# Up product with seven short products in pairs 5 to 21, their banks in turn by pair

## The reference

```
    h = _rmsnorm(x, g_pre_ffn[i])
    u = _causal_dwconv(h @ w_up[i], w_conv[i], b_conv[i])
    a, v = u[..., :D_FF], u[..., D_FF:]
    x = x + _rmsnorm((jax.nn.gelu(a) * v) @ w_down[i], g_post_ffn[i])
```

## Time and profile before

| | us |
|---|---|
| median of 3 runs | 1533.89 |
| lowest and highest run | 1531.69, 1535.56 |
| the profiled execution, its own time | 1533.2 |
| its span (first to last instruction) | 1531.3 |
| up product, pairs 4 to 21 (464.69 to 653.98) | 189.29 |

### The profile page before, as it was taken

The page is one execution under the profiler, slowest core; times in us unless marked ns, Lnnn a source line. Parts: engine busy times, 40 slices in busy tenths (PEclk is TensorE's granted clock), DMA queues, the critical chain, the costliest instruction groups (busy, mean ns, idle before and its releaser), DMA issues.

```text
span 1531.3 us, 20288 instructions
## 1 busy us (share of the span) xinstructions
PE 1491.1 (97%) x7953; PEld 1027.9 (67%) x7954; DVE 737.1 (48%) x1252; ACT 532.6 (35%) x975; POOL 556.4 (36%) x373
## 2 busy tenths in 40 slices
PE   8999999999999999999999999999999999999997
PEld 7975677888779999988888777468443443443433
DVE  4156765223785666623335778664533332332334
ACT  5246664223544544421246333424111111111112
POOL 3454555444447666544723362622100010010000
PEclk9999999999999999999999999999999999999999
DMA  8233002222103223352224222368999999999996
GB/s 314 98 110 95 2 2 97 96 97 97 69 33 114 103 83 110 111 188 98 98 84 128 88 81 69 110 250 309 359 429 430 428 427 430 430 429 426 425 425 245
DMA packets 52641, 306.95 MB, mean 200 GB/s; under 512 B 7097, under 2 KB 7353, under 8 KB 40000
## 3 DMA queue, kind: packets, MB, share of 16 engines
q1 hardware_dynamic: 47872, 292.03, 48.8%
q0 software_dynamic: 4096, 11.49, 2.0%
q10 hardware_dynamic: 576, 2.10, 0.3%
HBM read 303.39 MB, written 4.19 MB: 201 GB/s over the span
## 4 chain that ended last, share of the span: by engine, by line
PE 82%; DMA 7%; DVE 7%; ACT 1%; POOL 1%; issue 1%; SPq 0%; DVEq 0%; ACTq 0%
PE banks L535 14%; PE banks L1360 13%; PE banks L580 12%; DMA ring<-experts 7%; PE banks L538 7%; PE banks L1406 5%; PE banks L2693 4%; PE banks L1415 3%; PE banks L2696 2%; PE banks L560 2%; PE banks L2599 2%; PE banks L1160 2%; PE banks L2583 2%; PE banks L2665 1%; PE banks L2569 1%; PE banks L1018 1%
## 5 line engine op out<-in xcount | busy, mean ns | idle before, releaser
L498 POOL TENSOR_TENSOR arena_r<-ring,arena_r 128x1024 fp32r<-128x1024 f32 x125 | 311.9, 2502 | 317.4 <-ACT arena_r L483 297.9
L483 ACT ACTIVATE arena_r<-ring 128x1024 fp32r<-128x1024 f32 x125 | 131.4, 1058 | 320.9 <-PE banks L538 144.3
L1360 PE MATMUL banks<-ring,arena 128*64 128x512 f32 x704 | 223.7, 608 | 12.7 <-DMA ring<-experts 12.7
L535 PE MATMUL banks<-hT_r,arena_r 128*128 128x512 f32 x496 | 194.4, 392 | 0.7 <-ACT arena_r L483 0.4
L535 PE MATMUL banks<-arena_r 128*128 128x512 f32 x496 | 193.3, 390 | 0.0
L580 PE MATMUL banks<-arena_r 128*128 128x512 f32 x784 | 183.5, 389 | 0.6 <-DVE arena_r L525 0.6
L580 PEld LDWEIGHTS banks<-arena_r 128*128 128x128 f32 x784 | 147.1, 188 | 31.6 <-POOL arena_r L498 1.0
L1360 PEld LDWEIGHTS banks<-ring,arena 128*64 128x64 f32 x704 | 70.4, 140 | 144.4 <-issue 143.3
L855 POOL MEMSET arena<- 128x1024 f32 x15 | 14.3, 952 | 340.5 <-PE banks L1313 331.5
L2053 DVE TENSOR_TENSOR resid<-resid,banks 128x1024 f32<-128x1024 f32 x60 | 70.6, 1218 | 129.1 <-PE banks L1415 129.1
L1360 PE MATMUL banks<-arena 128*64 128x512 f32 x278 | 115.9, 595 | 0.0
(11 more groups left out here) (540 smaller groups left out, 2624.1 us busy)
## 6 DMA issues: line engine op xcount, KB each, us to landing
ring<-stream SPq DMA_DIRECT2D x164, 512.0 KB, 3.3
arena<-experts SPq DMA_DIRECT2D x35, 2048.0 KB, 15.9
ring<-experts SPq DMA_DIRECT2D x32, 2048.0 KB, 15.2
ring<-experts SPq DMA_DIRECT2D x17, 1024.0 KB, 18.1
arena<-experts SPq DMA_DIRECT2D x31, 512.0 KB, 11.4
arena<-experts SPq DMA_DIRECT2D x11, 1024.0 KB, 17.3
ring<-experts SPq DMA_DIRECT2D x14, 512.0 KB, 6.8
hT<-experts SPq DMA_DIRECT2D x8, 512.0 KB
```

The costliest lines, as they stand in the source:

```text
L483: nc.scalar.activation(parts(name, m)[:, 0, :], tile(tile_n), ACT.Copy).then_inc(S["w_high"], 1)
L498: nc.gpsimd.tensor_tensor(w[:, 1, :], tile(tile_n), plain(w[:, 0, :]), ALU.subtract).then_inc(S["w_low"], 1)
L535: nc.tensor.matmul(pb[:, bank, :], w[:, 0, k * P:(k + 1) * P], b[:, k, :], start=(k == 0 and part == 0), stop=False)
L1360: last = nc.tensor.matmul(pb[r, bank, :], XT[:, k, r], weights(b, c + e, k * 512, (k + 1) * 512), start=(k == 0), stop=(k == ND - 1))
```

## The change

Mixed are now all pairs from j = 4 to j = 20; plain are 0 to 3 and 21. Pairs 5, 7, ... 19, eight of them, go from plain to mixed. Every pair j, plain or mixed, uses banks 0 to 3 if j is even and 4 to 7 if it is odd. Behind a mixed pair the terms are rounded in their natural order 0 to 6. The token sums t1 to t4 are split one pair later on DVE. The down product starts with token tiles 0, 1 instead of 2, 3.

```diff
-MIXED = range(FIRST_MIXED, NF, 2)
+MIXED = range(FIRST_MIXED, NF - 1)
...
-TERM_ORDER = [4, 5, 6, 0, 1, 2, 3]
+BEHIND_PLAIN, BEHIND_MIXED = [4, 5, 6, 0, 1, 2, 3], list(range(7))
 NQ = len(TERMS)
+
+
+def term_order(j):
+
+    return BEHIND_MIXED if j - 1 in MIXED else BEHIND_PLAIN
...
+        def up_bank(j, w):
+
+            return pb[:, 4 * (j % 2) + w, :]
+
         def term_bank(j, q):
 
             bank, half = PLACES_OF[q]
-            return pb[:, 4 + bank, 256 * half:256 * half + 256]
-
-        def up_bank(j, w):
-
-            if j in MIXED:
-                return pb[:, 4 + w, :]
-            return pb[:, 2 * (PLAIN.index(j) % 2) + w, :]
...
+                if j >= 2:
+                    pe.wait_ge(S["up_dve"], 2 * (j - 2) + 2)
                 if j in PLAIN:
-                    if j >= 2:
-                        pe.wait_ge(S["up_dve"], 2 * PLAIN[PLAIN.index(j) - 2] + 2)
                     for w in range(2):
-                        split_features(pe, "up", 2 * j + w, 2 * (PLAIN.index(j) % 2) + w, hT_r, up_low, 2)
+                        split_features(pe, "up", 2 * j + w, 4 * (j % 2) + w, hT_r, up_low, 2)
                     continue
-                if j > FIRST_MIXED:
-                    pe.wait_ge(S["up_dve"], 2 * (j - 2) + 2)
                 for q in range(NQ - 1):
                     if TERMS[q].split()[1] in ("t1", "t2", "t3"):
                         pe.wait_ge(S["up_sums"], summed(TERMS[q].split()[1], "low"))
                     up_term(j, q).then_inc(S["up_part"], 1)
                 pe.wait_ge(S["up_sums"], summed("t4", "low"))
                 up_term(j, NQ - 1).then_inc(used, 2)
-            split_tokens(pe, "down", S["post_mm"], ((2, 3), (0, 1)), lambda q: pe.wait_ge(S["up_g"], NF - 1 + q))
+            split_tokens(pe, "down", S["post_mm"], ((0, 1), (2, 3)), lambda q: pe.wait_ge(S["up_g"], NF - 1 + q))
...
             def term_high(j, q):
-                if q < 4:
+                if q < 4 and j - 1 in PLAIN:
                     act.wait_ge(S["w_used"], W_UP + 2 * (j - 1) + (1 if q < 2 else 2))
                 elif j == FIRST_MIXED:
                     act.wait_ge(S["w_used"], W_UP)
-                elif q < NQ - 1:
-                    act.wait_ge(S["up_part"], terms_done(j - 2, q))
                 else:
-                    act.wait_ge(S["w_used"], W_UP + 2 * (j - 2) + 2)
+                    before = max(other for other in MIXED if other < j)
+                    act.wait_ge(*((S["up_part"], terms_done(before, q)) if q < NQ - 1 else (S["w_used"], W_UP + 2 * before + 2)))
...
+            for j in range(NF):
+                if j in MIXED:
+                    for q in (6, ) if j - 1 in MIXED else (2, 3):
+                        term_high(j, q)
+                elif j - 1 in PLAIN:
+                    high_act(act, "up", 2 * j + 1)
+                for w in (0, 1) if j - 1 in MIXED else (1, ) if j else ():
+                    conv_last(j - 1, w)
+                if j == 1:
                     x_high("t1")
                     x_high("t2")
-                high_act(act, "up", 2 * j + 3)
-                conv_last(j, 1)
-                gelu(j)
-                if j == 1:
-                    act.wait_ge(S["w_low"], made(W_UP + 3))
+                if j in PLAIN and j + 1 in MIXED:
+                    for q in (4, 5, 6):
+                        term_high(j + 1, q)
+                if j:
+                    gelu(j - 1)
+                if j == 2:
                     x_high("t3")
                     x_high("t4")
-            for q in TERM_ORDER[:5]:
-                term_high(FIRST_MIXED, q)
-            conv_last(FIRST_MIXED - 1, 0)
-            for j in MIXED:
-                for q in TERM_ORDER[5:]:
-                    term_high(j, q)
-                conv_last(j - 1, 1)
-                gelu(j - 1)
-                take_first(j)
-                for w in range(2):
-                    high_act(act, "up", 2 * j + 2 + w)
-                if j + 2 in MIXED:
-                    for q in TERM_ORDER[:3]:
-                        term_high(j + 2, q)
-                for w in range(2):
-                    conv_last(j, w)
-                gelu(j)
-                if j + 2 in MIXED:
-                    for q in TERM_ORDER[3:5]:
-                        term_high(j + 2, q)
+                if j in MIXED:
+                    take_first(j)
+                if j == NF - 1:
+                    high_act(act, "down", 0)
+                elif j + 1 in MIXED:
+                    for q in (0, 1) if j in PLAIN else range(6):
+                        term_high(j + 1, q)
                 else:
-                    high_act(act, "down", 0)
-                conv_last(j + 1, 0)
+                    for w in range(1 if j in PLAIN else 2):
+                        high_act(act, "up", 2 * j + 2 + w)
+                if j in PLAIN:
+                    conv_last(j, 0)
...
                 if j > FIRST_MIXED:
-                    dve.wait_ge(S["w_low"], term_made(j - 2, TERM_ORDER[-1]))
+                    before = max(other for other in MIXED if other < j)
+                    dve.wait_ge(S["w_low"], max(term_made(before, q) for q in (2, 3, 5)))
...
+            for j in range(NF):
+                if j == 2:
                     x_low("t1")
                     x_low("t2")
-                conv(j, 1)
-                gated_rows(j)
-                if j == 1:
+                if j == 3:
                     x_low("t3")
                     x_low("t4")
-            weight_sums(FIRST_MIXED)
-            conv(FIRST_MIXED - 1, 0)
-            for j in MIXED:
-                conv(j - 1, 1)
-                gated_rows(j - 1)
-                for what in ("c11", "u2", "u4", "u3", "c12", "c22", "c21"):
-                    join(j, what)
-                if j + 2 in MIXED:
-                    weight_sums(j + 2)
-                for w in range(2):
-                    conv(j, w)
-                gated_rows(j)
-                if j + 2 not in MIXED:
+                if j - 1 in MIXED:
+                    join(j - 1, "c21")
+                if j in PLAIN and j + 1 in MIXED:
+                    weight_sums(j + 1)
+                for w in (0, 1) if j - 1 in MIXED else (1, ) if j else ():
+                    conv(j - 1, w)
+                if j:
+                    gated_rows(j - 1)
+                if j in MIXED:
+                    join(j, "c11")
+                    if j + 1 in MIXED:
+                        weight_sums(j + 1)
+                    for what in ("u2", "u4", "u3", "c12", "c22"):
+                        join(j, what)
+                if j == NF - 1:
                     dve.wait_ge(S["up_g"], 2)
-                    dve.wait_ge(S["w_low"], term_made(j, TERM_ORDER[-1]))
+                    dve.wait_ge(S["w_low"], split_at(W_UP + 2 * max(MIXED)))
                     split_dve(dve, chain, "down", gT, 0, 2)
-                conv(j + 1, 0)
+                if j in PLAIN:
+                    conv(j, 0)
```

More of the change, by code:

```diff
@@ L146 @@
 TERMS = ["gate_1 x_1", "gate_2 x_2", "s2 t2", "s1 t1", "s3 t3", "s4 x_4", "value_2 t4"]
-TERM_ORDER = [4, 5, 6, 0, 1, 2, 3]
+BEHIND_PLAIN, BEHIND_MIXED = [4, 5, 6, 0, 1, 2, 3], list(range(7))
 NQ = len(TERMS)
+def term_order(j):
+    return BEHIND_MIXED if j - 1 in MIXED else BEHIND_PLAIN
 SUMS = ["s1", "s2", "s3", "s4"]
-UP_SUMS = [(t, "whole") for t in ("t1", "t3", "t2", "t4")] + [(t, "low") for t in ("t1", "t2", "t3", "t4")] + [(FIRST_MIXED, s) for s in SUMS]
-for _j in MIXED:
-    UP_SUMS += [(_j, c) for c in ("c11", "u2", "u4", "u3", "c12", "c22", "c21")] + [(_j + 2, s) for s in SUMS if _j + 2 in MIXED]
+UP_SUMS = [(t, "whole") for t in ("t1", "t3", "t2", "t4")] + [(t, "low") for t in ("t1", "t2", "t3", "t4")]
+for _j in range(FIRST_MIXED - 1, NF):
+    UP_SUMS += [(_j - 1, "c21")] if _j - 1 in MIXED else []
+    UP_SUMS += [(_j + 1, s) for s in SUMS if _j in PLAIN and _j + 1 in MIXED]
+    if _j in MIXED:
+        UP_SUMS += [(_j, "c11")] + [(_j + 1, s) for s in SUMS if _j + 1 in MIXED] + [(_j, c) for c in ("u2", "u4", "u3", "c12", "c22")]
 HIGHS = []
@@ L158 @@
     elif (_n - W_UP) % 2:
-        HIGHS += [(_j, q) for q in TERM_ORDER]
+        HIGHS += [(_j, q) for q in term_order(_j)]
 PLACES_OF = [(0, 0), (0, 1), (1, 0), (1, 1), (2, 0), (2, 1), (3, 0)]
@@ L175, in split_at @@
     j = (n - W_UP) // 2
-    return term_made(j, TERM_ORDER[-1]) if W_UP <= n < W_DOWN and j in MIXED else made(n)
+    return term_made(j, term_order(j)[-1]) if W_UP <= n < W_DOWN and j in MIXED else made(n)
 def summed(*what):
@@ L414, in build @@
         first_term, second_sum, third_sum, fourth_sum = [junk[:, 256 * q:256 * q + 256] for q in range(4)]
+        def up_bank(j, w):
+            return pb[:, 4 * (j % 2) + w, :]
         def term_bank(j, q):
             bank, half = PLACES_OF[q]
-            return pb[:, 4 + bank, 256 * half:256 * half + 256]
-        def up_bank(j, w):
-            if j in MIXED:
-                return pb[:, 4 + w, :]
```

(18 more changed lines are left out.)

3 lines of the change are left out of this document (removed).

## The result

The changed kernel takes 1541.86 us (median of 4 runs, 1540.28 to 1543.1) against 1533.77 for the kernel before in the same comparison (4 runs, 1531.69 to 1535.56). The ratio is 1.0055, interval 1.0043 to 1.0067: 8 us slower, with eight pairs more on the cheaper form of the product. (Pairs are numbered from 0 throughout: the mixed ones are now 4 to 20.) The up stage, from its first matmul to the first one of the down product, went from 234.29 us (419.69 to 653.98) to 243.30 (418.12 to 661.42), +9.0. What lies behind it takes 877.3 us before and 877.5 after. The stretch ahead of it was 1.6 us shorter in this execution; over the profiled executions of this document the stage starts between 418.01 and 421.40 us, so that difference isn't put down to the change.

The account below looks back on a forecast made before the run. The prediction took the path shared by POOL's low parts and DVE's two-SBUF-operand instructions as the new bound, 11.3 us a pair against PE's 10.07. 1533.2 + 8.6 = 1541.8, beside the runs' median 1542.5, rounded up to 1543 us; range 1534 to 1551.

Parts of the forecast that it names:

- The price of a pair: Steady mixed pairs: a period of 11.3 us, against 10.07 us of PE.
- The layout of the shared path: Seven POOL low parts and five DVE instructions of a mixed pair, excluding each other, laid out in turn: 11.3 us.
- the gap: No weight sum ran beside POOL in the trace; the skill's rule was used to assume that they collide.
- The stage: Up stage, counted by DVE: down product starts at 662.6 instead of 653.98, +8.6 us.
- the sum: Whole kernel: profiled execution's 1533.2 plus 8.6 for the up stage, 1541.8 us.
- the sign that I named: Mixed pairs: PE waiting about 1.2 us a pair for POOL's low parts (L2292).
- The other sign: PE's pairs 10.1 us apart at first and 11.3 from about pair 9.
- The gain that was promised: Up stage if PE stays the bound: 6.7 us from eight pairs plus 0.7 at the start, 7.4 us.
- Sums that slip past POOL: Rival: in mixed pairs only the gated product collides, PE bounds, 7.4 us gained, 1526.5 us; chance 0.14.
- Milder collisions: Rival: some sums of a mixed pair find POOL idle, period 10.5 to 11.0, 1531 to 1538.5 us; chance 0.12.
- Worse ones: Rival: POOL also gets in between s2, s3 and s4, period 13.6, +35 us, 1578 us; chance 0.06.

Follow-up runs that it names:

- e2: Changed kernel with the four weight sums reading their second operand from PSUM instead of SBUF, up product not computed: 1526.09 us, ratio 0.9948.
- e7: Changed kernel with plain pairs 8, 13 and 18 put in among the mixed ones: 1532.09 us, ratio 0.9996 against the kernel before.
- e6: Changed kernel with POOL making only the first 256 of 512 elements of each low part, work left out: 1525.13 us, ratio 0.9955.
- e3: Changed kernel with ACT writing the gelu into PSUM, where DVE's gated product reads it: 1533.42 us, ratio 1.0001 against the kernel before.
- e8: Changed kernel with the gelu written to PSUM and plain pairs 9 and 15 among the mixed ones: 1526.75 us, ratio 0.9959.

## Why the prediction was right

**The price of a pair.** The layout of the shared path gave 11.3 us; it measured 11.34, in each of 15 periods within 0.02. Its parts hold one by one: expected waits 0.6 (gated product), 0.7 (s1), 1.0 (s2), measured 0.66, 0.76, 0.98; s3, s4, joins and convolutions unchanged. That the weight sums had never met POOL in the trace was the gap; e2 closes it by moving one operand, and the Trainium skill's rule ("SBUF — State Buffer", "Who interferes with whom": two SBUF inputs on DVE against a GpSimd instruction that reads SBUF) agrees with the rows of this case: sums with one SBUF operand kept their length beside POOL (0.68 us in e2); where one with two overlapped a POOL instruction, one of the two was longer than alone, in all 70 such meetings of the changed kernel between 424 and 680. The Trainium skill, on the same page "SBUF — State Buffer", section "SBUF: two separate sides", adds that the one that starts first gets the shared pair of ports for the whole instruction and the other fully blocks. The rows above agree: POOL shuts DVE out for 1.16 us of its row of 1.30, and DVE shuts POOL out for 0.54 us of its row of 0.69.

**The stage.** Expected +8.6 us, measured +9.0. The first join of pair 4 came 48.8 us after the stage's start, not 49.7 (the stops at the start were worth 1.38 us in pairs 0 to 3, where the prediction took 0.7); the first period was 12.62, not 12.5; fifteen periods made 170.1, not 169.5; and PE was done with pair 20 0.9 us after its first join, not 0.3. The small errors cancel in part. The profiled execution took 1540.66 us where the sum has 1541.8, since the stretch ahead ran 1.6 us shorter, which the change doesn't explain. So it is in part luck that the time came out within a microsecond of the sum; the stage, 0.4 off, owes nothing to that. Counting by DVE and not by PE was the step that mattered: PE runs through the first pairs at 10.1 us on the lead it has, and a count of 16 x (11.34 - 10.08) from the first mixed pair would have put 20 us against 8 x 0.83 saved, 13.5 instead of 9.

**PE's waits.** Here the sign that I named was only half right. I expected about 1.2 us of them a pair, for POOL's low parts (L2292); the view names 0.36 for these and 0.42 for ACT's rounded copy (L2930), which I had not named, and ACT in turn waits 4.35 us for DVE's s2. The whole loss is in those two places all the same. From start to start PE's matmuls of 256 columns are 0.12 us apart; at the two stops (574.59 and 576.13) and behind them the steps are 0.70, 0.19, 0.64 and 0.22, 1.27 more, and the period is 1.26 longer than PE's 10.08. The view shows less, since a matmul's row runs on for 0.28 us. The wait of ACT and the two stops of one period:

```profile
573.81 1.15 ACT L2930 ACTIVATE arena_r<-arena 128x512 fp32r<-128x512 f32 x2 [4.35 <-DVE arena L3278]
...
574.59 1.18 PE L2701 MATMUL banks<-ring_r,arena_r 128*128 128x256 f32 x8 [0.42 <-ACT arena_r L2930]
...
576.13 0.75 PE L2704 MATMUL banks<-ring_r,arena_r 128*128 128x256 f32 x4 [0.36 <-POOL arena_r L2292]
```

The other sign, that pairs come 10.1 us apart at first and 11.3 from about pair 9, is borne out: the steady stops begin at 508.07, in pair 8.

**The gain that was promised** is real and was measured in e2: 17 mixed pairs without the collisions give a stage of 225.88 us, 8.4 under the kernel before (7.4 was my figure, and 1526.5 the time that I gave this rival): 1.4 in pairs 0 to 3 and 7.0 in pairs 4 to 20. The changed kernel needs 17.4 us more than that, and so loses the gain and 9.0 besides.

**The rivals.** Sums that slip past POOL: excluded by the rows of s1 and s2. Milder collisions: excluded by the period. Worse ones, between s2, s3 and s4: s3 and s4 at 678 and 679 ns exclude them, for the reason given, that POOL waits there (1.35 us) for the copy of s2.

**What stays open.** Whether another order of the terms behind a plain pair, or weights fetched sooner, would take the stops out of e7 was not tried. The runs show which instructions shut each other out and for how long, not in what part of the chip. e2 and e6 leave work out, so their times are bounds and not kernels to use; e3 and e8 compute everything and carry the same account. The run-to-run spread (1530.74 to 1538.22 us over the runs of the kernel before in one comparison) is as large as the effect; the verdicts rest on the ratios, the mechanism on the rows.

## What to carry to other kernels

When DVE and POOL both fit into a stage by their own sums, add up one more: POOL's instructions plus DVE's instructions with two operands in SBUF, as if they were one engine; if that is longer than the stage's bound, expect it to be the bound. Start-to-start times added up give somewhat too much (11.8 us here against 11.34); laying the order out gives the rest. Such a sum says nothing of a chain of waits where the pattern changes, as at the seams of e7. A row of one engine that is longer than its like, with no idle time beside it, is where to look for it, and moving one operand to PSUM takes the instruction out of the sum. A saving a pair can be taken for as many pairs as the helpers can keep up with: here 15 of 17 with one collision removed.

## What the runs showed of the hardware

- Where both had such an instruction waiting, they took turns in every period read here: a DVE instruction of 512 elements (two SBUF operands) held POOL up for 0.54 us, POOL's of 512 kept DVE out for 1.16 us from its start, and DVE never waited through two of POOL's. Whether POOL would get in between two of DVE's is open: POOL had nothing to do when s3 and s4 started.
- POOL's instructions follow each other every 1.25 us, but DVE got the path after 1.16 (worked out from the rows of both). The simple sum 7 x 1.25 + 5 x 0.61 = 11.8 is therefore too high, by 0.5.
- Reading the second operand from PSUM costs DVE nothing: 0.68 us for 512 elements either way, with the same 256 columns read twice.
- POOL's instruction of half the length (256 elements) takes 0.73 or 0.74 us, not 0.65, starts 0.70 apart.
- Busy time of DVE and POOL counts time spent shut out. DVE's 96% in the changed stage had 2.4 us of waiting in each 11.34.
